# Moving the loads of the modulation matrix from the synchronisation engine's DMA queue to GpSimd's

## What is computed

```python
def first_block(x, c, ...):
    c_act = jax.nn.silu(c)
    mod = (c_act @ w_mod[l] + b_mod[l])[:, None, :]
    sh1, sc1, g1, sh2, sc2, g2 = jnp.split(mod, 6, axis=-1)
    h = rmsnorm(x, norm1_w[l]) * (1.0 + sc1) + sh1
    x = x + g1 * mixer(h, rel_bias, w_in[l], ...)
    h = rmsnorm(x, norm2_w[l]) * (1.0 + sc2) + sh2
    x = x + g2 * swiglu(h, w_ffn_in[l], w_ffn_out[l])
    return rmsnorm(x, final_norm_w)

def reference(x, c, ...):
    x = first_block(x, c, ...)
    return second_block(x, p_2, ...)
```

## Time and profile before

| | |
|---|---|
| time, three runs | 3454.26 us median (3443.43 to 3458.05) |
| the profiled execution | 3449.73 us, of which the span from first to last instruction is 3447.9 us |
| PE busy | 3271.7 us, 95% of the span |
| DVE busy | 2344.2 us, 68% |
| ACT busy | 1428.4 us, 41% |
| POOL busy | 0.2 us |
| moved by DMA | 693.13 MB, 201 GB/s on the mean |

### The profile page before, as it was taken

How to read it: one execution, slowest core, us unless ns; L and a number is a source line. 1 busy time by engine, 2 the same in 40 slices (tenths; PEclk the granted TensorE clock), 3 DMA queues, 4 the chain that set the end, 5 groups by cost and what they waited for, 6 DMA issues and landing times.

```text
span 3447.9 us, 53921 instructions
## 1 busy us (share of the span) xinstructions
PE 3271.7 (95%) x22959; PEld 3015.2 (87%) x22959; DVE 2344.2 (68%) x2889; ACT 1428.4 (41%) x1357; POOL 0.2 (0%) x4
## 2 busy tenths in 40 slices
PE   6999999999999999899999999888989999999999
PEld 4788988989998898788888788788989999999988
DVE  6587467778777877767776555668855576555666
ACT  3233554543544343333333333345456444534333
POOL 0000000000000000000000000000000000000000
PEclk9999999999999999999999999999999999999999
DMA  8787544457444766466665455543544443445554
GB/s 334 311 312 258 196 156 159 171 196 292 172 159 159 308 247 241 156 234 234 236 222 197 173 188 187 185 159 135 188 170 146 148 171 144 161 173 208 204 188 159
DMA packets 105668, 693.13 MB, mean 201 GB/s; under 512 B 10991, under 2 KB 14127, under 8 KB 31188
## 3 DMA queue, kind: packets, MB, share of 16 engines
q1 hardware_dynamic: 97776, 655.30, 51.9%
q10 hardware_dynamic: 7652, 34.37, 2.7%
HBM read 679.05 MB, written 13.72 MB: 201 GB/s over the span
## 4 chain that ended last, share of the span: by engine, by line
PE 75%; DVE 13%; ACT 3%; DVEq 3%; issue 3%; DMA 2%; ACTq 0%; SPq 0%
PE accp L477 22%; PE accp L478 12%; PE accp L482 10%; PE accp L483 10%; PE accp L484 10%; DVE wlo L1476 3%; DVE cv L1766 2%; PE accp L480 1%; DMA raw<-w 1%; DVEq L1765 1%; PE pw L541 1%; DVE hrec L1515 1%; ACT whi L1009 1%; DVE dec L1784 1%; PE pw L733 1%
## 5 line engine op out<-in xcount | busy, mean ns | idle before, releaser
L1476 DVE TENSOR_TENSOR wlo<-raw,whi 128x2048 fp32r<-128x2048 f32 (+1 forms) x544 | 1200.3, 2210 | 504.0 <-ACT whi L1009 499.8
L1009 ACT ACTIVATE whi<-raw 128x2048 fp32r<-128x2048 f32 (+1 forms) x544 | 1003.0, 1847 | 642.3 <-DMA raw<-w 613.3
L482 PE MATMUL accp<-act,whi 128*128 128x256 f32 x3744 | 1086.3, 290 | 16.8 <-DVE wlo L1476 8.6
L483 PE MATMUL accp<-act,whi 128*128 128x256 f32 x3744 | 1066.5, 285 | 0.0
L484 PE MATMUL accp<-act,wlo 128*128 128x256 f32 x3744 | 1066.1, 285 | 0.0
L482 PEld LDWEIGHTS accp<-act,whi 128*128 128x128 f32 x3744 | 726.1, 194 | 25.4 <-ACT gl L1019 9.7
L483 PEld LDWEIGHTS accp<-act,whi 128*128 128x128 f32 x3744 | 726.3, 194 | 5.8 <-issue 5.3
L484 PEld LDWEIGHTS accp<-act,wlo 128*128 128x128 f32 x3744 | 725.5, 194 | 0.0
L477 PE MATMUL accp<-act,whi 128*128 128x512 f32 x1890 | 674.0, 399 | 4.3 <-ACT tf L1019 4.3
L478 PE MATMUL accp<-act,wlo 128*128 128x256 f32 x2016 | 546.1, 281 | 0.0
L477 PEld LDWEIGHTS accp<-act,whi 128*128 128x128 f32 x1890 | 356.1, 188 | 85.8 <-ACT tf L1019 4.5
(11 more groups left out here) (465 smaller groups left out, 3910.6 us busy)
## 6 DMA issues: line engine op xcount, KB each, us to landing
raw<-w SPq DMA_DIRECT2D x480, 1024.0 KB, 4.8
raw<-w SPq DMA_DIRECT2D x64, 704.0 KB, 4.0
mraw_a<-wm SPq DMA_DIRECT2D x38, 1024.0 KB, 9.6
mraw_b<-wm SPq DMA_DIRECT2D x24, 1024.0 KB, 7.0
mraw_c<-wm SPq DMA_DIRECT2D x16, 1024.0 KB, 6.9
mraw_x<-wm SPq DMA_DIRECT2D x10, 1024.0 KB, 14.6
acb<-ac_d ACTq DMA_DIRECT2D x8, 1024.0 KB, 4.7
mraw_w<-wm SPq DMA_DIRECT2D x8, 1024.0 KB, 7.2
```

Source lines behind the costliest of these rows:

```text
L482: pe.matmul(acc[:, 0:S], wh, x2[:, 0, :], start=first, stop=False)
L483: pe.matmul(acc[:, 0:S], wh, x2[:, 1, :], start=False, stop=False)
L1009: act.activation(whi[:, c % 4, 0:k, :], raw[:, c % 4, 0:k, :], ACT.Copy).then_inc(hi_done, 1)
L1476: dve.tensor_tensor(wlo[:, c % 4, 0:k, :], raw[:, c % 4, 0:k, :], whi[:, c % 4, 0:k, :].bitcast(F32), ALU.subtract).then_inc(lo_done, 1)
```

## The change

All 96 pieces are issued by GpSimd, which has its own DMA queue and nothing else to do. SP keeps the chunks and the inputs. GpSimd waits for `xT` to land before m0. Each piece waits for its free slot as before, and four pieces for the memory of their buffers (`MREADY` in the place of `MWAIT`). Pieces from m32 on are no longer tied to a chunk. The order of work on TensorE, VectorE and ScalarE is untouched.

```diff
-        MWAIT = {C0["sp0"] + 3: (grp, 5), C0["sp1"] + 3: (grp, 9), C0["fi"] + 3: (used, 2 * C0["fi"])}
+        MREADY = {48: (grp, 5), 60: (grp, 9), 72: (used, 2 * C0["ap"]), 80: (used, 2 * C0["fi"])}
...
         @block.sync
...
-            def piece(m):
...
             for q in range(4):
-                for m in range(8 * q, 8 * q + 8):
-                    piece(m)
-                    if m % 8 == 5:
-                        load(C0["qs"] + 3 * q)
-                for g in range(1, 3):
+                for g in range(3):
                     load(C0["qs"] + 3 * q + g)
             for c in range(C0["qkv"], CHUNKS):
                 load(c)
-                if c in MWAIT:
-                    sp.wait_ge(*MWAIT[c])
-                for m in MPIECE.get(c, ()):
-                    piece(m)
...
+        @block.gpsimd
+        def _(pool):
+            pool.wait_ge(x_in, 16)
+
+            def piece(m):
+
+                for a, b, _, ring in MSTAGES:
+                    if 32 <= m and 4 * a <= m < 4 * b:
+                        pool.wait_ge(mod_used_d, 8)
+                        pool.wait_ge(mod_used, max(32, 4 * a, m - ring + 1) - 8)
+                if 6 <= m < 32:
+                    if (m - 6) % 4 == 0:
+                        pool.wait_ge(mod_used_d, (m - 6) // 4 + 1)
+                    else:
+                        pool.wait_ge(mod_used, 3 * ((m - 6) // 4) + (m - 6) % 4)
+                b = MORDER[m // 4]
+                pool.dma_start(mod_slot(m), wm[one(b), m % 4].rearrange("a p k n -> p (a k) n")).then_inc(mod_landed(m)[0], 16)
+
+            for m in range(96):
+                if m in MREADY:
+                    pool.wait_ge(*MREADY[m])
+                piece(m)
```

## The result

| | before | after |
|---|---|---|
| time, 20 runs each | 3452.43 us median (3443.43 to 3459.53) | 3458.42 us median (3451.01 to 3468.48) |
| ratio after / before | | 1.0019, 95% interval 1.0011 to 1.0028 |
| the profiled execution | 3449.73 us, span 3447.9 | 3459.13 us, span 3457.3 |

The change makes the kernel slower by 0.19%: 0.0019 x 3450 = 6.6 us, with 3 us to either side. That is inside what the prediction called no change and close to its +6.0. The sum was nearly right, but not its terms, as the traces show. In the code after, lines that stand behind the edit have moved by two (L541 is now L543, L1009 is L1011), and in the experiments by other amounts; GpSimd issues its pieces at L451.

The account below looks back on a forecast made before the run. TensorE was taken as busy for 3271.7 of 3447.9 us, with transfers bounding the kernel only where they crowd together. Start +3.5 and m14 +2.5 gave +6.0 on 3454.3, about 3460 us; range 3446 to 3475.

Parts of the forecast that it names:

- "+3.5 us" at the start: Kernel start: chunks sharing the engines make m3 late, and the norm's chain up to `mod_block(1)` moves with it, +3.5 us.
- I take equal halves: Kernel start: pieces and chunks in flight together each get half the transfer rate, so landings come in pairs every 5 us.
- pieces go first, about +9: Bound at the start: second `ple` chunk lands behind six pieces, 15 us later, about +9; as a rival 3464 to 3470, chance 0.10.
- "+2.5 us" at m14: Piece m14, issued at 73.01 us without slack: chunk qs5 shares the engines and doubles its transfer, +2.5 us.
- "0, at most +7.5" for the bursts: Stages from `qkv` on: four pieces issued at once when a stage opens cost 0, at most +7.5 us.
- the bound of 2.5: Each of three bursts: a whole burst ahead of a chunk delays it 10 us, of which 2.5 would show.
- the cover: `sp0`: chunk 4's rest is ready at 761.0, TensorE starts on it around 768.5, so 7.5 us of delay are free.
- "0" for the wait taken from SP: SP's queue no longer blocks before pieces and qs4 loads from 60 to 73 us: 0, at most -2 us.
- "`x` at `wo`": Reload of `x` at `wo`: taking away the pieces before and after it gives 0, at most -1 us.
- the two queues together move less than one: Rival, whole kernel: two queues working together lower the transfer rate, +15 us at 350 GB/s; chance 0.13.
- GpSimd's queue is held up by VectorE: Rival, m1 to m3 and m14: pieces start only between VectorE's instructions, +4 to +9 on the sum, 3464 to 3469; chance 0.08.
- Hidden after all: Rival: start and m14 cost little, or the unblocked queue gives it back; sum -2 to +3, 3452 to 3457 us; chance 0.27.

Follow-up runs that it names:

- e4: Changed kernel, but only pieces m0 to m31 stay on GpSimd's queue; m32 to m95 go back to SP in the old order: 3452.92 us, ratio 1.0006.
- e9: e4 with one wait added: SP issues chunk qs5 only once piece m15 has landed: 3451.70 us, ratio 1.0005 to the kernel before.
- e6: Changed kernel without GpSimd's wait for `xT` before its first piece: 3470.93 us, ratio 1.0054 to the kernel before.
- e1: Changed kernel with four idle products put on TensorE between m13 and m14 of block 3: 3457.34 us, ratio 1.0014 to the kernel before.
- e5: Changed kernel, but GpSimd holds each piece from m32 on until the chunk it was tied to before: 3454.28 us, ratio 1.0011 to the kernel before.
- e2: Changed kernel, but SP loads chunk qs5 only when m14 and m15 have landed: 3453.06 us, ratio 1.0004 to the kernel before.
- e7: Changed kernel with the edits of e5 and e2 together: 3447.48 us, ratio 0.9993 to the kernel before; a second set gave 3446.78 us, ratio 0.9988.

## Why the prediction was right, and where it wasn't

The forecast (+3 to +9, about +6 us, within 0.5% of before) and the range held. The interval of 1.0011 to 1.0028 is clear of 1, so there is a loss, but one of 0.2%. By its steps:

- **"+3.5 us" at the start: wrong, in sign.** The step that failed is "I take equal halves". Shares went by packets, and the pieces with packets of 7.4 KB got 77% of the bytes against chunks with 2.2 KB. m3 wasn't late: TensorE was through with it at 31.2 and not 34.8, and `mod_block(1)` started at 44.41 and not near 48. The -3.2 us that showed instead are no transfer time but go with the place and length of a slow stretch of TensorE's clock, of which the prediction had no word; e4 and e9 have the same loads and, in their traces, -1.2 and +0.5. The bound "pieces go first, about +9" was wrong too: the second `ple` chunk came 1.5 us later (16.98 against 15.51) and not 15, since it was ahead of the pieces in time of issue. e6 shows what that bound was afraid of, once GpSimd doesn't wait for `xT`.
- **"+2.5 us" at m14: right in its place and its wait (2.77 us), mis-sized by what follows.** The pair of m13 and m14 took 7.25 us (72.84 to 80.09) where some 6 were forecast. A slow stretch can follow the wait: the step is +8.5 and +8.8 us in two traces, +2.7 to +2.8 in the three others that have the late landing (e1, e5, e6). By the runs the place is worth 5 to 8 us in two pairs of kernels (after and e2, e5 and e7) and 0.4 in a third (e4 and e9).
- **"0, at most +7.5" for the bursts: wrong value, and in each of the two stages the bound of 2.5 was passed.** The failed step is the cover: it was measured to TensorE's start, "7.5 us of delay are free", and passed over VectorE, which has work for nearly all of the stage and had waited 0.50 us for this rounding already. The chunk came only 4 us late, well inside those 7.5, and all of it showed. Measured by trace +4.0 and +4.1 us at `sp0` and `sp1` (3.7 to 4.8 in all ten steps of the five kernels that burst from GpSimd's queue, -1.2 to +1.2 in the ten of the five that don't burst). By the runs it is 3 to 7 us for both.
- **"0" for the wait taken from SP: right.** No step of any trace shows a gain where SP's queue was freed; that qs4 now loads between 60 and 73 us (DMA share 0.43, 0.07 before) gave nothing to be seen either.
- **"`x` at `wo`": 0, at most -1.** The lag falls by some 2 to 3 us around there in all kernels but e5, with pieces on either queue, so nothing can be said.

Of the rivals, "the two queues together move less than one" is refuted: 417 GB/s from 5 to 30 us against 420 before, and a share of 1.01 there. "GpSimd's queue is held up by VectorE" has nothing for it: an issue takes 0.53 us wherever it stands, m1 to m3 were on time while VectorE worked, and m14's packets start when qs5 has moved. e7 shows m14 at 5.04 us on the same queue with the chunk gone. The rule of the Trainium skill in "DMA: Bandwidth & Descriptors", section "SWDGE vs HWDGE vs iDMA", that spreading issues saves only the time to initiate them, fits: full stretches moved 417 GB/s against 420, and what changed was which load came first. "Hidden after all" describes e2 and e5 better than the kernel after.

So the right answer came in part by luck: one term of +3.5 that was -3 by the trace, and two places of 2.5 and 0 that were 8.5 and 8.1 by the trace after (by the runs 0 to 8 and 3 to 7).

What stays open: what m14 is worth by the runs, since e4 and e9 don't bear out the other pairs; why the clock fell right behind m14's wait in two traces (waits of 2.77 and 2.94 us) and not in e5 and e6 (2.65 and 2.64 us, nothing in the gap), while at the start 2.41 us were followed by a slow stretch; what decided that qs5 and m14 moved in turn and not by turns; and why the steps of the traces at the bursts (8 us) are larger than what the runs give for them (3 to 7), though the intervals of 3 us to either side can hold both.

## What to carry to other kernels

When loads move to a second queue, the old queue's order was also a pace. Write down for each place where both queues become ready at the same moment who is late behind whom, and follow the late chunk through every engine that must touch it: the one with the least idle time, here VectorE, sets the cover and not the last one. Keep the pace with a wait (e7: pieces tied to their old chunks, and one chunk held back until the piece that has no slack has landed) and the second queue cost nothing here (-2.4 and -4.1 us in two sets). And a wait of 2 to 3 us ahead of dense products has two prices, its own length and a stretch at 1.2 GHz that may or may not follow, so that single profiles differ by more than the edit under study (e5's was 7 us under the median of its runs).

## What the runs showed of the hardware

- Two queues with transfers in flight together moved equal numbers of packets (686 to 695 from 14 to 30 us), so the queue with packets of 7.4 KB got 77% of the bytes against one with 2.2 KB.
- A transfer that comes while the other queue's is under way may see nothing move for 3 to 4 us: m14 issued at 70.08 and moving from 74.1, the chunk issued at 754.85 and moving from 758.3. With nothing in its way m14 moved after 1.2 us (e7).
- TensorE's clock went to 1.2 GHz behind idle times of 2.4 to 3.2 us, for as long as some 15 us (2 us windows from 80 to 94 us, after, all at 0.50), and in e5 not right behind 2.65 us: there it held until 86 us.
- The time of a run follows its mean clock: over the 20 runs after, 0.976 goes with 3468.48 us and 0.982 with 3451.01, about 2.4 us for 0.001 (correlation -0.86). It is the larger part of this kernel's scatter.
